# A two-block network on one core: low parts moved ahead in the merges, second gate row behind the first down products, the delta mixer's projection by token tiles

## The reference

```python
# first network, each of two layers
h = rmsnorm(x, norm_mix)
(...) = split_cols(h @ w_in)                  # the inputs of four branches, and gate_logits
gates = sigmoid(gate_logits).reshape(b, s, 4, 1024)
branches = (y_a, y_b, y_c, y_m)               # conv, sparse attention, recurrence, memory attention
merged = gates[:, :, 0] * (branches[0] @ w_lift[0])
for n in range(1, 4):
    merged = merged + gates[:, :, n] * (branches[n] @ w_lift[n])
x = x + merged @ w_out
hf = rmsnorm(x, norm_ffn)
gate, up = split(hf @ ffn_w_up, 2)
x = x + (silu(gate) * up) @ ffn_w_down

# second network, two layers; g1, g2, shifts and scales come from c (the modulations)
a = modulate(h, norm1_w, sh1, sc1)
m = ab_mixer(a, ac, ...)      # layer 0: delta rule and gated linear attention; ends in  y @ w_out
m = hyena_mixer(a, ...)       # layer 1: long convolutions
h = h + g1 * m
h = h + g2 * swiglu(modulate(h, norm2_w, sh2, sc2), w1, w3, w2)
```

## Time and profile before

| | |
|---|---|
| time, median of 3 runs | 2290.32 us (2289.24 to 2291.94) |
| the profiled execution: span | 2290.6 us (the profile gives no time of its own besides) |
| PE busy | 2186.0 us, 95% |
| PE weight loads busy | 1873.6 us, 82% |
| DVE busy | 1432.1 us, 63% |
| ACT busy | 808.9 us, 35% |
| read from HBM | 345.21 MB, 151 GB/s over the span |
| mean granted clock of PE | 0.970 |

### The profile page before, as it was taken

One profiled execution on the slowest core, in us unless ns is written; L12 is line 12 of the kernel. 1 busy time (PEld: TensorE's weight loads), 2 busy tenths in 40 slices (PEclk: granted clock), 3 DMA queues, 4 the chain that ended last, 5 costly groups with the idle time before them and its releaser, 6 DMA issues.

```text
span 2290.6 us, 36110 instructions
## 1 busy us (share of the span) xinstructions
PE 2186.0 (95%) x15182; PEld 1873.6 (82%) x15182; DVE 1432.1 (63%) x2369; ACT 808.9 (35%) x1026; POOL 57.3 (3%) x79
## 2 busy tenths in 40 slices
PE   6999899999999989999999998989899999999997
PEld 5997799799999868978997787876599977557996
DVE  4891667599568536758975385665477662645444
ACT  3453542333335445214443253220344312104342
POOL 0000000000000000000100000000100000000000
PEclk9999899999999989999999998998999989999999
DMA  7442347776464333687873212010686433204552
GB/s 223 163 152 106 110 158 253 235 249 210 139 197 148 129 111 111 219 281 237 297 254 100 81 67 74 2 39 1 193 269 223 153 120 110 74 10 147 185 184 74
DMA packets 207766, 348.59 MB, mean 152 GB/s; under 512 B 20642, under 2 KB 111561, under 8 KB 207220
## 3 DMA queue, kind: packets, MB, share of 16 engines
q1 hardware_dynamic: 192704, 290.89, 37.9%
q0 software_dynamic: 14624, 55.31, 7.0%
q10 hardware_dynamic: 276, 0.08, 0.0%
HBM read 345.21 MB, written 1.05 MB: 151 GB/s over the span
## 4 chain that ended last, share of the span: by engine, by line
PE 83%; DVE 12%; ACT 3%; issue 1%; DMA 1%; SPq 0%; DVEq 0%; ACTq 0%
PE psum L447 35%; PE psum L841 29%; PE psum L484 15%; DVE G L1348 2%; DMA ring<-in_w_in_dram 1%; PE psum L819 1%; PE psum L542 1%; PE psum L556 1%; DVE wide_room L1348 1%; DVE A L1348 1%; DVE ring_low L1218 1%; DVE ring_low L1348 0%; ACT A L944 0%; DVE x L1348 0%; DVE A L1727 0%
## 5 line engine op out<-in xcount | busy, mean ns | idle before, releaser
L1218 DVE TENSOR_TENSOR ring_low<-ring,high_weights 128x2048 fp32r<-128x2048 f32 x124 | 284.2, 2292 | 137.9 <-ACT high_weights L1211 135.2
L841 PE MATMUL psum<-high_rows,high_weights 128*128 128x256 f32 x1280 | 361.9, 283 | 0.0
L841 PE MATMUL psum<-high_rows,ring_low 128*128 128x256 f32 x1280 | 361.2, 282 | 0.0
L484 PE MATMUL psum<-mix_rows_high,ring_low 128*128 128x256 f32 x960 | 272.4, 284 | 0.0
L447 PE MATMUL psum<-hT,ring 128*128 128x128 f32 (+1 forms) x1552 | 256.8, 328 | 9.6 <-DVE x L1348 3.5
L447 PEld LDWEIGHTS psum<-hT,ring 128*128 128x128 f32 x1552 | 231.9, 197 | 33.1 <-issue 5.8
L841 PEld LDWEIGHTS psum<-high_rows,ring_low 128*128 128x128 f32 x1280 | 243.6, 190 | 0.0
L841 PEld LDWEIGHTS psum<-high_rows,high_weights 128*128 128x128 f32 x1280 | 241.3, 189 | 2.5 <-issue 1.2
L1211 ACT ACTIVATE high_weights<-ring 128x2048 fp32r<-128x2048 f32 x124 | 237.9, 1918 | 5.5 <-PE psum L841 1.7
L484 PEld LDWEIGHTS psum<-mix_rows_high,ring_low 128*128 128x128 f32 x960 | 184.6, 192 | 0.0
L841 PE MATMUL psum<-x2T_low,high_weights 128*128 128x256 f32 x640 | 180.4, 282 | 0.0
(11 more groups left out here) (443 smaller groups left out, 3787.8 us busy)
## 6 DMA issues: line engine op xcount, KB each, us to landing
ring<-in_w_in_dram SPq DMA_DIRECT2D x36, 2048.0 KB, 7.8
ring<-in_ffn_w_dram SPq DMA_DIRECT2D x66, 1024.0 KB, 5.3
ring<-in_ffn_w_up_dram SPq DMA_DIRECT2D x44, 1024.0 KB, 6.4
A<-in_mod_w_dram POOLq DMA_DIRECT2D x40, 1024.0 KB, 7.4
ring<-in_ffn_w_down_dram SPq DMA_DIRECT2D x22, 1024.0 KB, 5.0
ring<-in_w_lift_dram SPq DMA_DIRECT2D x16, 1024.0 KB, 9.1
ring<-in_ab_w_in_dram SPq DMA_DIRECT2D x7, 2048.0 KB, 8.2
ring<-in_hy_w_in_dram SPq DMA_DIRECT2D x6, 2048.0 KB, 8.3
```

The lines of the kernel that those rows point to most:

```text
L484: ins = pe.eng.matmul(out, lhs[a], rhs[b], start=first and n == 0, stop=last and n == 2)
L841: ins = pe.eng.matmul(out, lhs[a], rhs[b], start=first and n == 0, stop=last and n == 2)
L1218: v.eng.tensor_tensor(low, whole, high.bitcast(F32), ALU.subtract).then_inc(*v.mark(f"w_lo/{l}.{i}"))
```

## The change

Three edits, each of which moves instructions and adds none.

1. In the branch for the memory keys, `lows(l, "gate{}.0.1", 1)` is called right behind `newton`, so the low part of the panel's fourth part is made there, in both layers of the first network.
2. The call of `spread` for the second gate row moves on PE from behind the products of step 0 to behind the down products of panel 0, and on ACT from step 0 to step 1, in `ffn2` and `ffn3`.
3. `mixed_out` takes its four parts by token tile (tile 0 both halves, then tile 1), and `mixed_norm` for layer 0 does its adds in that order, with tile 0's norm behind its second add and `norm_out` of tile 0 behind the third.

```diff
@@ ffn_tensor
                             if t:
                                 ins.then_inc(*pe.mark(labels[g], [used]))
-                    if l in top["gate_spread"]:
-                        top["gate_spread"][l]["pe"]()
                 elif j < FFN_STEPS:
...
                     for t in range(MT):
                         ins = down_product(i, t, wh, wl)
                     ins.then_inc(*pe.mark(f"down_done/{l}.{i}", [used]))
+                    if i == 0 and l in top["gate_spread"]:
+                        top["gate_spread"][l]["pe"]()
@@ ffn_act
-            if j == 0 and l in top["gate_spread"]:
+            if j == 1 and l in top["gate_spread"]:
                 top["gate_spread"][l]["act"]()
@@ dve_program, first network
             lows(l, "gate{}.0.1", 0)
             v.wait_ge(*reached(f"mk_rs0/{l}"))
             newton(None, A2[:, 0:1024], A3[:, 0:1024], A1[:, 1024:2048])
+            lows(l, "gate{}.0.1", 1)
             tt(mkT[:, :, :], mkT[:, :, :], A2[:, 0:1024].rearrange("p (h t) -> p h t", h=4), ALU.mult, f"mkT/{l}")
@@ mixed_out
-            parts = [(half, t) for half in range(2) for t in range(MT)]
+            parts = [(half, t) for t in range(MT) for half in range(2)]
@@ mixed_norm
-            for half in range(2):
-                for t in range(MT):
-                    if half and t:
-                        norm_rows(key, 0, x)
-                        norm_out(key, 0, gain_, shift)
-                    mixed_add(l, half, t)
+            by_rows = [(half, t) for t in range(MT) for half in range(2)]
+            by_half = [(half, t) for half in range(2) for t in range(MT)]
+            for half, t in (by_rows, by_half)[l]:
+                if (half, t) == ((0, 1), (1, 1))[l]:
+                    norm_rows(key, 0, x)
+                if (half, t) == (1, 1):
+                    norm_out(key, 0, gain_, shift)
+                mixed_add(l, half, t)
```

## The result

The changed kernel took 2271.38 us (median of 4 runs, 2268.39 to 2276.36), the kernel before beside it on the same chip 2291.13 us (4 runs, 2289.24 to 2294.26): the ratio is 0.9909, with a 95% interval of 0.989 to 0.9928. Forecast were 2272 us. The profiled execution after took 2271.08 us with a span of 2269.3 us; its mean granted clock was 0.975, that of before 0.970.

The account below looks back on a forecast made before the run. PE bounds the kernel (95% busy), so time is won only where it stands still or runs at its lower clock. 5.2 + 7.0 + 2.4 + 3.7 = 18.3 us off 2290.3 gives 2272 us, range 2267 to 2278.5.

Parts of the forecast that it names:

- Layer 0's unit: Merges of layer 0, fourth gate-panel part: stall of 3.65 us goes, 1.54 us of clock comes back, 5.2 us.
- layer 1's: Merges of layer 1, fourth part: 4.71 us stall and 2.37 us of clock, less 0.1; taken as 7.0 us.
- DVE's lag in layer 1: Layer 1 merge: DVE, no longer idle, reaches the reduction 7.0 us earlier, taking 0.1 us off the gain of 7.1.
- upper bound of 12.2: Both merge units together: stalls alone give 8.4 us, stalls and clock 12.2 us.
- DVE takes over: Rival, merges: the next low parts come late as DVE slips, up to 2 us per layer lost, 2275; chance 0.08.
- Projection: Delta mixer's projection by token tiles: the xn stall goes and the first feed-forward product starts 2.75 us earlier.
- Projection and first row together: Up to ffn2's down products: 2.4 us gained where 4.6 were possible, as modulation data hold back the low part.
- how much earlier the data come: ffn2: modulation data taken to come 0.6 us earlier, at 1660.25, putting the low part at 1667.3.
- later release of the projection's first panel: Loads before ffn2: panel freed behind the third part, not the second, so two weight panels move 3.5 us later.
- `ffn3`: 3.7 forecast: Gate row in layer 3's feed-forward: 2.0 us of waiting and 1.7 us of clock come back.
- The rival on the clock: Lower clock falls anyway or elsewhere, so 5.6 us of clock are not given back: 2278; chance 0.17.
- signs of being wrong: Profile after: a new wait over 3 us before a following merge unit, or slow stretches as many as before.

Follow-up runs that it names:

- e1: Kernel before with only the fourth part's low part moved right behind the Newton steps, in both layers' merges: 2277.87 us, ratio 0.9936.
- e5: Kernel before with that low part moved only half way up, behind the scans, leaving a short stall: 2282.91 us, ratio 0.9966.
- e6: Changed kernel with the first part's three low parts also made ahead of the memory queries' mean square: 2270.81 us, ratio 0.9914.
- e3: Kernel before with only the projection by token tiles, DVE's residual adds following: 2287.14 us, ratio 0.9985.
- e9: Changed kernel measured and profiled once more, no new lines: 2271.37 us, ratio 0.9915.
- e2: Kernel before with only the second gate row moved behind the first down products, in ffn2 and ffn3: 2287.5 us, ratio 0.9978.
- e7: Changed kernel with the edits of e4 and e6 together: 2269.97 us, ratio 0.9912.
- e8: The kernel of e4 measured and profiled once more, no new lines: 2271.68 us, ratio 0.9911.
- e4: Changed kernel with POOL issuing ffn2's first modulation load ahead of the next mixer's constants: 2267.77 us, ratio 0.9898.
- e10: Changed kernel with the gate row of ffn2 back in its old place, that of ffn3 left in the new one: 2273.81 us, ratio 0.9922.

## Why the prediction was right

The forecast of 18.3 us met 19.75. The mechanisms of the merges and the projection, 15 us of it, came out as told. Those of the two rows did so in part, and one reason, that the projection's change holds back the loads of `ffn2`, is not borne out. That the sum is so near has luck in it: the profiled pair has -2.97 us ahead of all edits and 3.36 us right behind the merges' units, for which the forecast had no term.

**Layer 0's unit: 5.2 forecast, 5.45 measured; layer 1's: 7.0, measured 7.57.** The stalls went whole and the clock stayed at 1.00 behind them (e1, alone, the same). DVE's lag in layer 1, 0.1 us, did not occur: it waits 0.41 us for PE at the reduction. What is over is a size. 0.23 us in layer 1 was gained from 867 to 883: the lower clock had reached past the 24 products that I counted. The other 0.26 us stands in both layers, and e5 shows it twice more: its stalls of 1.05 and 0.91 us cost 1.30 and 1.17 us against a unit without one (5.45 - 4.15, 7.56 - 6.39). A wait of PE costs about 0.25 us more than the idle time in its row, and the sum had no term for that. With both, the two units gained 13.0 us, above the upper bound of 12.2. "DVE takes over" was seen nowhere in the changed kernel (its price, 2 us per layer, makes 2276 and not 2275); e6, which asks a little more, runs into it.

**Projection: in full.** 2.75 us from the distance of the chain of DVE, measured 2.77 (e3 alone 2.76). The `hT` wait of 1.2 us was 1.34.

**Projection and first row together: 2.4 forecast, 3.2 measured (2.77 + 0.43), and 2.63 in e9.** As told, PE waits for `ring_low` before the down products in place of the row's wait, 1.42 and 2.05 us where about 2 were forecast, and behind it DVE waits for the modulation data, 3.34 and 3.97 us. The mis-sized term is how much earlier the data come than in before: forecast 0.6 us, measured 1.6 us (0.9 in e9), as DVE reached the modulation 2.77 us earlier and waited 1.2 us (1.8) longer.

The reason given for the delay was the later release of the projection's first panel. The traces don't bear it out. With the projection as before DVE waited 2.15, 2.91 (e2), 4.31 (e1) and 4.32 us (e5); with it changed and the load in its old place, between 3.34 and 3.97 us in five traces. From POOL's issue of the load to DVE's start it took 11.7, 12.6, 13.9 and 14.0 us in the first four, 12.9 to 13.5 us in the other five. The profiled execution of before had the shortest of all, so a comparison with it alone shows a delay that executions of the same code show as well. What made its load quick is open.

That the data hold PE up in the changed kernel is shown by e7 and e8: with the data first, 1.7 to 2.2 us return. The panels are not out of it: in e4 the same edit brought nothing, since the panel came late. And that the two edits compete for the same slack is not shown: by e2 the row alone gained 0.38 us in `ffn2`, by e10 and e3 between -0.2 and 0.3 us beside the projection's change, both at the wait for the same load. What the row's new place does bring there is the slow stretch that stood behind the old one in four of five traces.

The Trainium skill (DMA: Bandwidth & Descriptors, Issuing engines are not separate DMA queues) says that loads of SP and of GpSimd share the engines. The traces of e4 and e7 agree: with POOL's load first, ACT waits 7.12 and 5.21 us for SP's panel, 2.86 us in the changed kernel. That of e8 shows no such price (3.46 us against 3.50 in e9). The two together fill 354 GB/s in the changed kernel.

**`ffn3`: 3.7 forecast, 3.45 measured, but half of it is there only in part of the executions.** The wait of 1.72 us went with the row, 3.45 - 1.56 = 1.9 us by the starts. The 1.7 us of clock I had put down to the stall. e1 and e3 leave the row alone and get 1.56 us too: with the same 0.31 and 1.72 us of waiting as before, no slow stretch stood there, while e5 had it as before did. Two of four executions with the old place had it in `ffn3`, none of eight with the new one. So as a part of the time of the change the term was too high, by about half of the 1.6 us if two of four is the share (an estimate from four traces); in the pair of profiles it was right. In `ffn2` the forecast had no such term, as the one trace of before had no slow stretch there, and four of the five traces with the old place had one. The two errors go against each other.

**The rival on the clock** had a chance of 0.17. It failed where it was priced most: in both merges the lower clock went with the stall, and in 9 traces with a fourth-part stall of at most 1.05 us there was none behind it. But in the rest of the program it is true in both directions: slow stretches stood at other places in nearly every trace, from 883 to 900 (gain of 1.69, or loss of 3.21 in e1), in `ffn2` (none, or 1.6 us in e1, e3, e10, where the row's waits stand), ahead of 245.7 (5.2 us between e8 and e9). These sums are as large as the smaller terms of the forecast. The Trainium skill (TensorE: Matmul & The Clock Gate, Part 1: The HAM clock gate) has the window in which the gate looks at PE run free of the kernel, which fits that the same code met a clock of 0.84 and 0.92.

Of the forecast's signs of being wrong none came: no new wait over 3 us stood before a merge unit, and between 150 and 2250 us there were 17 slow stretches in each of the changed kernel's two traces, 21 in that of before.

**What stays open.** Why the load of the modulation took 11.7 to 14.0 us in executions of the same code. Which of the kernels e4 and e6 to e9 is best: their medians (2267.8 to 2271.7) are within each other's intervals. And why the low stretches ahead of 245.7 differ between executions.

## What to carry to other kernels

An operand that was ready long before its product is the surest gain: find the instruction on the releasing engine, look back for the time at which its inputs were there, and move it there; check that what it passes has more slack than its own length. A stall on PE often costs clock behind it as well, so price both, but weigh the clock by the share of executions that show the slow stretch behind the same stall; one profile gives it in full or not at all. Take more than one profile of the kernel before, too: here its only one had the quickest load of a stage and no slow stretch in it, and every comparison with it inherits that. When an edit starts a stage earlier, ask which load the stage waits for: the row's move in `ffn2` gained at most 0.43 us until that load was issued first, and then 2.08 us in two of three executions.

## What the runs showed of the hardware that was not expected

How steady the work is and how unsteady the clock: layer 0's unit gained 5.44 to 5.46 us in eight traces of six kernels, `ffn3` 3.44 to 3.46 us in eight, while the same kernel's timed runs spread over 8.4 us (e9) and that of before over 2285.72 to 2295.44 us in 11 runs. Whether the lower clock follows a stall does not go with the stall's length alone. Counted is a slow stretch that begins during the wait or at most 1.3 us behind it:

| wait of PE | us | slow stretch |
|---|---|---|
| merges, fourth part | 3.54 to 4.71 | 6 of 6 |
| merges, fourth part (e5) | 0.91, 1.05 | 0 of 2 |
| merges, first part | 1.68 | 18 of 20 |
| merges, first part (e6, e7) | 0.37 | 2 of 4 |
| projection, `xn`, old order | 3.17 | 2 of 4 |
| row, old place | 0.31, then 1.72 | 6 of 9 |
| `ffn2`, first down product, row in its new place | 0.99 to 2.05 | 0 of 4 |

Where an edit took the wait away or moved it, no slow stretch began at its place: 0 of 16 at the fourth part, 0 of 8 in the projection, 0 of 15 at the row. What else decides is not shown.
